# Attention with a convolution beside it: conv products, turned probabilities and denominators in one ring of three PSUM banks, light blocks' scores in a bank of their own, centring on GpSimd

## What is computed

```python
a = a_val * jax.nn.sigmoid(a_gate)                      # before this stage
a = jax.nn.silu(layer_norm(causal_depthwise_conv(a, conv_w, conv_b), ln_g, ln_b))
...
score = jnp.where((key_pos[None, :] <= qpos[:, None])[None], score, -jnp.inf)   # before this stage
_, idx = lax.top_k(score, topk)                         # before this stage
s = jnp.einsum('bqhd,bqkhd->bqhk', qb, k_sel) * (HEAD_DIM ** -0.5)
p = jax.nn.softmax(jnp.where(valid[:, :, None, :], s, -jnp.inf), axis=-1)
o = jnp.einsum('bqhk,bqkhd->bqhd', p, v_sel)
...
return jnp.concatenate([a, o], axis=-1) @ w_out         # after this stage
```

## Time and profile before

| | |
|---|---|
| median of 3 runs | 2590.16 us (2589.67 to 2592.37) |
| profiled execution | 2592.61 us, span 2590.8 us |
| mean granted TensorE clock | 0.965 of full speed |
| busy, share of the span | TensorE 93%, weight loads 80%, VectorE 78%, ScalarE 65%, GpSimd 25% |
| the stage of the change | 386 to 630 us, 9.4% of the span |

### The profile page before, as it was taken

How to read it: one execution, slowest core, us unless ns; L and a number is a source line. 1 busy time by engine, 2 the same in 40 slices (tenths; PEclk the granted TensorE clock), 3 DMA queues, 4 the chain that set the end, 5 groups by cost and what they waited for, 6 DMA issues and landing times. The chain is left out here.

```text
span 2590.8 us, 37548 instructions
## 1 busy us (share of the span) xinstructions
PE 2412.0 (93%) x12649; PEld 2071.5 (80%) x12649; DVE 2029.2 (78%) x2588; ACT 1684.9 (65%) x1815; POOL 643.5 (25%) x481
## 2 busy tenths in 40 slices
PE   8989998986979999999999599998979999999997
PEld 8969978874867888888888499996867888888885
DVE  3788876776888999899988543547778998998886
ACT  3369836666227887888887465663147878887775
POOL 0105814353012222222221412121002222222223
PEclk9999999997988999999999699999979999999998
DMA  5502354324339699988898411114259699999994
GB/s 173 141 6 93 82 98 132 100 67 127 108 140 379 228 354 370 363 330 325 310 375 295 179 57 33 41 33 154 96 202 346 237 348 371 374 373 367 376 371 181
DMA packets 121517, 565.80 MB, mean 218 GB/s; under 512 B 23735, under 2 KB 32183, under 8 KB 72144
## 3 DMA queue, kind: packets, MB, share of 16 engines
q1 hardware_dynamic: 96304, 513.25, 54.8%
q0 software_dynamic: 25120, 51.36, 7.2%
HBM read 575.32 MB, written 73.28 MB: 250 GB/s over the span
## 5 line engine op out<-in xcount | busy, mean ns | idle before, releaser
L2197 DVE TENSOR_TENSOR e0wlo<-e0raw,e0whi 128x2048 fp32r<-128x2048 f32 x214 | 487.1, 2290 | 59.9 <-ACT e0whi L2045 59.9
L2045 ACT ACTIVATE e0whi<-e0raw 128x2048 fp32r<-128x2048 f32 x214 | 409.8, 1915 | 92.3 <-PE e0banks L94 78.3
L2197 DVE TENSOR_TENSOR e1wlo<-e1raw,e1whi 128x2048 fp32r<-128x2048 f32 x138 | 313.1, 2286 | 42.4 <-ACT e1whi L2045 42.4
L2045 ACT ACTIVATE e1whi<-e1raw 128x2048 fp32r<-128x2048 f32 x138 | 263.9, 1913 | 42.5 <-PE e1banks L94 36.4
L92 PE MATMUL e0banks<-e0whi,e0xh 128*128 128x512 f32 x576 | 231.1, 401 | 1.1 <-DVE e0xl L2202 1.1
L94 PE MATMUL e0banks<-e0whi,e0xl 128*128 128x512 f32 x576 | 226.4, 393 | 0.0
L93 PE MATMUL e0banks<-e0wlo,e0xh 128*128 128x512 f32 x576 | 225.9, 392 | 0.0
L2197 DVE TENSOR_TENSOR e_wu<-e1raw,e_wu 128x2048 fp32r<-128x2048 f32 x70 | 160.3, 2292 | 17.3 <-ACT e_wu L2045 17.3
L92 PE MATMUL odd_banks<-h2T_hi,odd_w_hi 128*128 128x348 f32 x480 | 171.5, 357 | 0.8 <-DVE h2T_lo L2517 0.5
L2045 ACT ACTIVATE e_wu<-e1raw 128x2048 fp32r<-128x2048 f32 x70 | 134.2, 1918 | 49.0 <-PE e1banks L94 30.1
L93 PE MATMUL odd_banks<-h2T_lo,odd_w_hi 128*128 128x348 f32 x480 | 155.1, 323 | 0.0
(11 more groups left out here) (516 smaller groups left out, 6875.2 us busy)
## 6 DMA issues: line engine op xcount, KB each, us to landing
e0raw<-in_moe_w_gate SPq DMA_DIRECT2D x72, 1024.0 KB
e0raw<-in_moe_w_up SPq DMA_DIRECT2D x72, 1024.0 KB
e0raw<-in_moe_w_down SPq DMA_DIRECT2D x72, 1024.0 KB
e1raw<-in_moe_w_gate SPq DMA_DIRECT2D x70, 1024.0 KB
e1raw<-in_moe_w_up SPq DMA_DIRECT2D x70, 1024.0 KB
e1raw<-in_moe_w_down SPq DMA_DIRECT2D x70, 1024.0 KB
qki_w_raw<-in_w_even SPq DMA_DIRECT2D x22, 512.0 KB, 5.8
pre<-in_conv_band SPq DMA_DIRECT2D x32, 320.0 KB, 3.0
```

Of the source, the lines that this page charges most:

```text
L2045: act.activation(w_hi[i], raw[:, i, :], ACT.Copy).then_inc(hi_done[i], 1)
L2197: dve.tensor_tensor(w_lo[i], raw[:, i, :], w_hi[i].bitcast(F32), ALU.subtract).then_inc(lo_done[i], 1)
```

## The change

The change keeps every computation and every transfer, and moves where and when they happen.

- `c_ps` is gone and `t_ps` has three banks. Conv products, turned groups, denominators, means and variances use the three in turn, in the order in which TensorE issues them (`ring_order`); each use waits until the use three places earlier has been read (`bank_free`).
- ScalarE takes a conv group between the early and the late groups of turned probabilities, no longer at the end of the round.
- Scores of blocks 0 to 3 (at most 400 keys) go to the third bank of `s_ps`; those of blocks 4 to 7 use the first two, block 8 all three. `scores(n)` waits only for the last earlier step that shares a bank.
- The means are computed in four parts, each as soon as its eight groups are done (rounds 8, 20, 32 and 44), and added up by VectorE; ScalarE's copy of the mean is gone. The variances are likewise added up by VectorE, part by part, in a tile of their own.
- The centring is done by GpSimd, four instructions between the splits of head 6 and the output weights' splits. Squares move from rounds 50 to 53 to 48 to 51, variances from 51 to 54 to 49 to 52, the root from 56 to 55, the scaling from 58 to 57, the tanh from 60 to 59. The last product stays in 61 to 64.
- The three banks of `t_ps` are cleared before the other initial values, and the first conv groups wait for that.

```diff
+MEAN_IN = {GROUP_ROUNDS[W4 * (t + 1) - 1 - FIRST_GROUPS] + 2: t for t in range(CT)}
-MEAN_AT, CENTRE_AT, VAR_AT, ROOT_AT, SCALE_AT, SWISH_AT, OUT_AT = (CONV_STEPS + n for n in (1, 6, 8, 13, 15, 17, 18))
+CENTRE_AT, VAR_AT, ROOT_AT, SCALE_AT, SWISH_AT, OUT_AT = (CONV_STEPS + n for n in (4, 6, 12, 14, 16, 18))
+T_RING = 3
...
+        uses += turned[:EARLY_GROUPS] + conv + turned[EARLY_GROUPS:] if late_conv(n) else conv + turned
+        for t, g in denominator_at(n):
...
+            uses.append(("turned", k))
...
+        if n in MEAN_IN:
+            uses.append(("mean", MEAN_IN[n]))
+        if VAR_AT <= n < VAR_AT + CT:
+            uses.append(("var", n - VAR_AT))
...
-        t_ps = [d.ps(f"t_ps{i}", [P, 512]) for i in range(2)]
+        t_ps = [d.ps(f"t_ps{i}", [P, 512]) for i in range(T_RING)]
...
-        c_ps = d.ps("c_ps", [P, 512])
...
+        def bank(*use):
+            return t_ps[nth_use[use] % T_RING]
...
+        def score_banks(b):
+            first, last = (2, 3) if WIDTH[b] <= 512 else (0, -(-WIDTH[b] // 512))
+            return range(first, last)
...
             for h in range(1, HEADS):
                 if h == HEADS - 1:
+                    pool.wait_ge(mean_done, CT)
+                    for t in range(CT):
+                        pool.tensor_tensor(tile(t), tile(t), every(mean), ALU.subtract).then_inc(cen_done, 1)
                     ahead.split_all(pool, out_hi, out_lo)
...
+            def bank_free(*use):
+                i = nth_use[use] - T_RING
+                kind, k = uses[i] if i >= 0 else ("none", 0)
+                if kind == "turned":
+                    pe.wait_ge(t_free, k + 1)
+                elif kind == "conv":
+                    pe.wait_ge(conv_done, k + 1)
...
+                else:
+                    pe.wait_ge(ready, 1)
...
-                if g >= FIRST_GROUPS:
-                    pe.wait_ge(conv_done, g)
+                bank_free("conv", g)
...
             def variances(t):
                 pe.wait_ge(sq_done, t + 1)
-                if t == 0:
-                    pe.wait_ge(mean_done, 1)
+                bank_free("var", t)
...
-                if n:
-                    pe.wait_ge(s_read, n)
+                before = [m for m in range(n) if set(score_banks(STEPS[m][1])) & set(score_banks(b))]
+                if before:
+                    pe.wait_ge(s_read, before[-1] + 1)
...
-                    pe.wait_ge(ready, 1) if k < 2 else pe.wait_ge(t_free, k - 1)
+                    bank_free("turned", k)
...
             def beside(n):
-                if n in GROUP_IN:
-                    take_conv(GROUP_IN[n])
-                if n == MEAN_AT + MEAN_STEPS:
-                    act.wait_ge(mu_mm, 1)
-                    act.activation(mean[:], c_ps[:, 0:NPH], ACT.Copy, scale=1.0 / CONV_CH).then_inc(mean_done, 1)
                 t = n - CENTRE_AT - 1
                 if 0 <= t < CT:
                     act.wait_ge(cen_done, t + 1)
...
                     o_lows(UNIT_OF[n - 1])
+                if n in GROUP_IN:
+                    take_conv(GROUP_IN[n])
                 if n + 1 < N:
                     p_high(n + 1, False)
...
+                t = MEAN_IN.get(n)
+                if t is not None:
+                    dve.wait_ge(mu_mm, t + 1)
+                    if t == 0:
+                        dve.tensor_scalar(mean[:], small("mean", 0), 1.0 / CONV_CH, None, ALU.mult).then_inc(mean_done, 1)
+                    else:
+                        dve.wait_ge(mean_done, t)
+                        dve.scalar_tensor_tensor(mean[:], small("mean", t), 1.0 / CONV_CH, mean[:], ALU.mult, ALU.add).then_inc(mean_done, 1)
+                t = n - VAR_AT
                 if 0 <= t < CT:
-                    dve.wait_ge(mean_done, 1)
-                    dve.tensor_tensor(tile(t), tile(t), every(mean), ALU.subtract).then_inc(cen_done, 1)
...
+            for i in range(T_RING):
+                ins = dve.memset(t_ps[i][:], 0.0)
+            ins.then_inc(ready, 1)
             dve.memset(den[:], 1.0)
             dve.memset(pT[:, :, 0, :, :].bitcast(F32), 0.0).then_inc(padded, 1)
-            for i in range(2):
-                ins = dve.memset(t_ps[i][:], 0.0)
-            ins.then_inc(ready, 1)
```

More of the change, by code:

```diff
@@ L962 @@
 AHEAD, EARLY_GROUPS, DEN_AFTER = 3, 2, 2
[L965 to L977 removed]
+ROUNDS = N + 3 * DEN_AFTER
 def denominator_at(n):
@@ L1152, in taps, with means @@
                 pe.wait_ge(band_loaded[s], 16 * (g // BAND_RING + 1))
-                if g >= FIRST_GROUPS:
-                    pe.wait_ge(conv_done, g)
+                bank_free("conv", g)
                 for k in range(SHIFTS):
                     a = PAD - k
-                    last = pe.matmul(conv_out(g), b_raw[:, s, k * P:(k + 1) * P], glu4[:, g, a:a + NPH], start=k == 0, stop=k == SHIFTS - 1)
+                    last = pe.matmul(small("conv", g), b_raw[:, s, k * P:(k + 1) * P], glu4[:, g, a:a + NPH], start=k == 0, stop=k == SHIFTS - 1)
                 last.then_inc(conv_mm, 1)
-            def means(gs):
-                pe.wait_ge(conv_done, CG)
-                for g in gs:
-                    last = pe.matmul(c_ps[:, 0:NPH], phase, group(g), start=g == 0, stop=g == CG - 1)
-                if g == CG - 1:
-                    last.then_inc(mu_mm, 1)
+            def means(t):
+                pe.wait_ge(conv_done, W4 * (t + 1))
+                bank_free("mean", t)
+                for i in range(W4):
+                    last = pe.matmul(small("mean", t), phase, group(W4 * t + i), start=i == 0, stop=i == W4 - 1)
+                last.then_inc(mu_mm, 1)
             def variances(t):
                 pe.wait_ge(sq_done, t + 1)
-                if t == 0:
-                    pe.wait_ge(mean_done, 1)
+                bank_free("var", t)
                 for i in range(W4):
-                    last = pe.matmul(c_ps[:, 0:NPH], phase, spare[:, t % 2, i, :], start=t == 0 and i == 0, stop=t == CT - 1 and i == W4 - 1)
+                    last = pe.matmul(small("var", t), phase, spare[:, t % 2, i, :], start=i == 0, stop=i == W4 - 1)
                 last.then_inc(var_mm, 1)
@@ L1223, in _ @@
             turned(0, False)
-            for n in range(N + 3 * DEN_AFTER):
-                three = n + 1 < N and len(key_groups(STEPS[n + 1][1])) > EARLY_GROUPS
+            for n in range(ROUNDS):
                 if n + AHEAD < N:
                     scores(n + AHEAD)
-                if n in GROUP_IN and not three:
+                if n in GROUP_IN and not late_conv(n):
                     taps(GROUP_IN[n])
@@ L1231, in _ @@
                     turned(n + 1, True)
-                if n in GROUP_IN and three:
+                if n in GROUP_IN and late_conv(n):
                     taps(GROUP_IN[n])
@@ L1239, in _ @@
                     denominators(t, g)
-                if MEAN_AT <= n < MEAN_AT + MEAN_STEPS:
-                    means(range((n - MEAN_AT) * CG // MEAN_STEPS, (n + 1 - MEAN_AT) * CG // MEAN_STEPS))
+                if n in MEAN_IN:
+                    means(MEAN_IN[n])
                 if VAR_AT <= n < VAR_AT + CT:
@@ L1292, in p_high @@
                     rows = key_rows(n)
-                    src = t_ps[k % 2][0:rows, 0:len(js) * P].rearrange("p (j q) -> p j q", q=P)[:, :, 0:q]
+                    src = bank("turned", k)[0:rows, 0:len(js) * P].rearrange("p (j q) -> p j q", q=P)[:, :, 0:q]
                     act.activation(pT[0:rows, n % 2, js[0]:js[-1] + 1, 0, 0:q], src, ACT.Copy).then_inc(p_hi_done, 1)
```

81 lines of the change are left out of this document (47 added, 34 removed).

## The result

The changed kernel has a median of 2597.43 us in 15 runs (2592.18 to 2600.13), the kernel before, run in turn with it, 2592.37 (2588.84 to 2598.11). The ratio is 1.0016 with a 95% interval of 1.0009 to 1.0023: 0.16% slower, some 4.2 us. The slowdown is clear of the noise, though smaller than the 0.2% that the prediction took for the limit of what can be told. The forecast was a gain of 2.6 us, and 2597.43 lies above the range.

What follows compares the result with a forecast made beforehand. TensorE was taken to set the pace early, ScalarE late, with the conv output ending the stage. +1.6 +2.9 −5.7 −1.0 −0.4 = −2.6 us gave 2590.0 against the profiled 2592.61, a median of 2587.6; range 2581.5 to 2593.0.

Steps and rivals of the forecast that it cites:

- they no longer bind: Behind round 55: GpSimd's lines no longer delay the last product; full ScalarE leaves 0.4 of the tanh's 2.35 us.
- Before round 43: Up to the last conv group: shorter waits save 4.3 us, three mean groups cost 5.85, so 1.6 us later.
- the ring: Three shared banks before round 43: conv products' waits of 1.8 us and denominators' waits of 1.9 us go.
- the score bank: Before round 43: the waits of scores on the previous minimum, 1.0 us, go.
- The start: First conv product waits for three clearings, about 1.5 us later; a band wait takes most up, 0.4 us lost.
- The mean groups: Three of four come before round 43, where TensorE is the bound, at 1.95 us each: +5.85 us.
- The square behind GpSimd: Rounds 48 to 50: TensorE waits 1 to 7 us for the square behind GpSimd's centring; round 50 begins 2.9 us later.
- What VectorE gets back: To round 55: centring off VectorE saves 3.7 us of TensorE's waits, a moved variance product 1.95: together −5.7 us.
- From there to the first tanh: Behind round 55: the ring's third bank saves 1.0 us of denominators' waits; the tanh, one round up, begins 2.35 earlier.
- The rival that ends on the other side: ScalarE stalls behind GpSimd's centring and VectorE's relief doesn't show: +6.3 us, 2596.5 us; chance 0.08.
- The first rival: Waits fall further: the third bank frees half the turned groups' waits and the square's wait is hidden; 2582.5 us, chance 0.30.
- The last: No wait is really shortened by the ring and means only move: sum +2.7 us, 2592.9 us; chance 0.12.

Runs made afterwards that it cites:

- g_conv_bank: The changed kernel with the last product one round earlier, but conv products, means and variances in their own bank, turned groups in the other two; stage 244.08 us.
- base: The changed kernel with the last product one round earlier, on which later variants stand; stage 243.92 us, ratio to the kernel before 0.9995.
- a_out_earlier: The changed kernel with the last product one round earlier, in rounds 60 to 63; stage 243.92 us, ratio to the kernel before 0.9995.
- sq_later_out_earlier: The changed kernel with the last product one round earlier and squares and variances back in their old rounds; stage 237.07 us, one run of 2583.15 us.
- g_centre_dve: The changed kernel with the last product one round earlier and the centring on VectorE; stage 238.65 us, ratio to the kernel before 0.9984.
- g_earlier: The changed kernel with centring on VectorE, a clearing wait per bank, rounds behind the mark two earlier, last product three; median 2579.48 us, ratio to before 0.9953.

## Why the prediction was wrong

The step that failed is the last one, the −0.4 for the tanh's earlier round with "they no longer bind": it had a round of tanh moved ahead of its last product cost 2.0 us of ScalarE's time, and left out that the tanh waits for the product two tiles back. The stretch grew by 6.0 us. All steps, with times counted from the stage's zero:

- **Before round 43** (+1.6 predicted): the mark is 2.2 us later, or 3.8 at the slower start. The pieces: the ring was put at −1.8 −1.9 and is worth −1.9; the score bank at −1.0, measured −0.6; the 4.4 us of the turned groups were rightly left at nothing, though not for the reason given: they didn't wait for the value products' low halves but for ScalarE's taking out of the conv group. The start was put at +0.4; the first scores are 3.0 later and the twelfth minimum 0.5, or 2.1 with the slower start. The mean groups then cost some 4.2 of the 5.85, as a remainder and if the terms add: 98.81 us from the minimum to the mark before, less 1.9 and 0.6, against 100.5.
- **The square behind GpSimd** (+2.9): it came as predicted in place and sign. GpSimd's first subtraction took 2.19 instead of 2.43, head 6 was split at 543.78, TensorE waited 3.76, inside the 1 to 7. VectorE's 16x16 minimum behind it comes at 554.94 us (550.04 before), 4.2 later from the stage's zero, against 4.5 predicted (+1.6 +2.9).
- **What VectorE gets back** (−5.7): at the 272-wide minimum, at 567.48 us (565.99 before), four steps on, the lag is 0.8 instead of a lead of 1.2, so it was −3.4, 2.3 short of the forecast. The waits of the earlier trace rows did go, but two of 0.72 and 1.31 us on VectorE remained. In their place stood a variance product at the lower clock, 3.25 us for 1.95, and a mean clock of 0.91 from 548 to 566 us, where it was 0.94 before.
- **From there to the first tanh** (−1.0 −2.35): measured −3.15. The size is about right. That the ring is the source of the 1.0 isn't shown: g_conv_bank takes 58.2 us from the mark to the first tanh, base 59.0. By the prediction's own terms the first tanh should have been 4.55 us earlier than before (−1.2 −1.0 −2.35, "near 579"); it was 2.35 earlier, at 582.13.
- **The stretch, "they no longer bind"** (+2.0, which made −0.4 of −2.35): this is the step that failed. The prediction looked at the tanh against ScalarE's fill and at the lines against the last product, each by itself. It never asked what the tanh waits for besides. The text ahead of it even says that "the last product stays in 61 to 64", and that the tanh moves; the distance between them, with two buffers in `conv_spare`, was never counted. The stretch took 27.76 − 21.80 = 6.0 us more. With the old distance, in a_out_earlier, it took 21.49: there not even the 2.0 came.

Together: the last product was forecast 2.6 us earlier and came 3.6 later. Of the miss of 6.2 us, 4.0 lie in the stretch, 2.0 in the relief of VectorE (2.3 short, with 0.3 made up by the square), 0.2 between. Whether the rest of the change is a gain isn't shown: a_out_earlier, which has all of it but this fault, ends its last product 1.6 us earlier than the kernel before in its trace, at the slower start, and by its runs can't be told from it.

The rival that ends on the other side had the stall of ScalarE as its mechanism, at 2596.5 us; its time is nearer by luck, for its reason was not what decided: the stall was there, and relief and the earlier tanh more than paid for it. It was however worth more than the forecast's 2.9: taking it away by sq_later_out_earlier gives 6.9 us of the stage, by g_centre_dve 5.3 (6.2 and 4.1 at the last product). A wait of 4.9 us that is taken away can give more than its own length. The first rival (waits fall further) fell, as the ring gave 1.9 us. The last (the change does nothing it says) fell for the stretch ahead of the mark, by g_conv_bank; behind the mark the ring's gain isn't shown, as said.

The neighbours that the prediction weighed, VectorE's scaling and GpSimd's split, did not meet in the changed kernel, since the split ended at 573.85 and the scalings took 1.22 us each but one of 1.42. In sq_later_out_earlier they met:

```profile
573.64 1.22 DVE L1439 TENSOR_TENSOR glu<-glu,conv_mean 128x1040 f32<-128x1040 f32 x1
```

```profile
573.56 3.57 POOL L1150 TENSOR_TENSOR k_lo<-pre,k_hi 128x1044 fp32r<-128x1044 f32 x1
```

GpSimd was the one that became longer, 3.57 instead of 2.43, and VectorE had its 1.22; in the next scaling, at 576.62 us, VectorE took 1.62. The Trainium skill, "GPSIMD Engine Reference", section "Specifications", has the two contend for the shared interfaces when VectorE's instruction has two SBUF inputs, as the scaling has; the trace agrees, and adds that the loser may be either. In the kernel before both lost: beside the centrings of 2.98, 2.30 and 3.39 us GpSimd's three one-input splits took 3.78, 3.85 and 3.73 instead of 2.8. What decides which of them waits, no run here settles.

What stays open: what makes the clock fall a second time at the start of some traces, 1.6 us at the twelfth minimum; how the 6.9 us of the square's wait divide between the wait, the clock, the tail and the rounds behind it; and whether an even earlier table than g_earlier's would be better, which wasn't tried.

## What to carry to other kernels

When one producer and one consumer share a ring of buffers across two engines, write down for each pair the distance in rounds between "reads the buffer" and "overwrites it", and move both ends together: a move of the earlier end alone can turn a hidden wait into one that all engines share. Look for it where *all* engines' busy time falls in the same window. And put an operation that waits on another engine into a round by which its input is done, even when it already stands last in its round: the same centring on GpSimd made the square wait 5.95 us, and the stage 6.9 us longer, two rounds too early; in its old place the square waited 1.04 us.

## What was not expected of the hardware

- A start of the conv products 1.9 us later cost 3.0 us by the first scores, since the 30 products behind it ran at a granted clock of 0.62 where it was 0.81 (386 to 395 us). They took 6.41 us instead of 5.24.
- The same instructions got a mean clock of 1.00 or 0.89 in the same 15 us of different runs, worth 1.6 us. TensorE's waits just ahead, 0.27 and 1.34 us, were the same in both.
- GpSimd's instruction lengthened beside VectorE's, from 2.43 to 3.57 us, with VectorE's unchanged at 1.22; elsewhere both lengthened.
- GpSimd's subtraction of 128x1040 took 2.19 us in four; its own two-input operation with another output type of 128x1044 takes 2.43.
